# Hybrid decoder trunk: GpSimd's gathers of u and v in the order of the slots that use them, and the last norm in three parts

## The chip, the cores and the metric

The kernel runs on one core of one Trainium2 chip. The metric is device time in microseconds, from the start to the end of the program. The engines are TensorE (PE), VectorE (DVE), ScalarE (ACT), GpSimd (POOL) and SyncE (SP); each runs its own instructions in order, and they wait for each other by semaphores. 16 DMA engines serve the queues of SP and GpSimd.

## The reference

The model is a decoder trunk: 512 tokens, width 1024, two layers, float32. A layer has three token mixers, merged by gates, and then a layer of single-neuron experts (PEER); a last RMS norm closes it.

```python
for l in range(DEPTH):
    h = rmsnorm(x, norm1_g[l])
    z = h @ w_in[l]                                 # pool | ssm | q | k | v | 3 gates
    y_pool, y_ssm, y_attn = ...                     # pooling, state space, windowed attention
    merged = g[0] * y_pool + g[1] * y_ssm + g[2] * y_attn
    x = x + merged @ w_out[l]
    h2 = rmsnorm(x, norm2_g[l])
    x = x + peer_ffn(h2, ...)
return rmsnorm(x, final_g)
```

In the expert layer each token scores 128 + 128 keys for each of 8 heads, and keeps the 16 best pairs of a head: 128 experts of 16384 for a token. For every chosen expert e it computes a = h2 . u_tab[e], and adds gate * gelu(a) * v_tab[e] to the token. u_tab and v_tab hold a row of 1024 floats (4 KB) for each expert.

## The kernel before

**Tiles and picks.** Tokens go in tiles of 128, one to a partition; two layers of four tiles make eight tiles (TILES), numbered 0 to 7. A tile has 128 picks: in pick k every partition takes its own k-th expert. So there are 1024 picks, u picks and v picks alike, and for each one GpSimd issues an indirect DMA (L897) that gathers 128 rows of u (512 KB), and another for v. Rows of u land in one of six buffers (`rows_u`, pick mod 6), rows of v in one of six others (`rows_v`).

For a u pick VectorE multiplies the row with the token and sums (L2080, the dot; it bumps `dotted`). After each group of eight dots ACT takes the gelu (L1419) and VectorE multiplies by the gates (L2091, `weighed`). For a v pick, PE sums: ACT writes a diagonal matrix of the eight-group's weights (L1399, `diag_of`), and PE multiplies it with the rows of v into PSUM (L1147, `sum_pick`, two halves of 512 columns, each two matmuls in the trace). Some picks VectorE sums itself, into `tile_sum` (L1782; the first of a tile L1779). When a sum is done it bumps `v_free` of its buffer. At the end of a tile comes the "drain": VectorE joins both sums (L2059), PE transposes them (L951), and VectorE adds them to the tokens xT (L2066, `x_home`).

**The plan.** The order of all work is written at build time by `make_plan` as a list of slots; a slot takes at most one u pick and one v pick, and beside them pieces of the dense work ("items": projections, attention, selection of experts and so on, for a half of 256 tokens at a time) as far as assumed costs allow. Every engine then walks through the same slots in order. A v pick stands in the slot about 12 after the slot of its u pick (LAG): u picks fill slots 203 to 1226, v picks 215 to 1238. Dense items end near slot 1000; thereafter only picks are left, and all their v sums are PE's, because `v_on` asks for `at < len(order)`, that is, for dense items still to come.

**The gathers.** GpSimd walks through `GATHERS`, made by `gather_order`: the u pick of slot s is sorted under s, the v pick of slot s under s - 4 (V_AHEAD). Ahead of a u gather it waits for the dot of the pick six before (`dotted`), ahead of a v gather for the sum of the pick six before (`v_free`). The queue is in order: what stands behind a waiting gather waits too.

**Other traffic.** SP loads weights into a ring of six pieces of 512 KB, each once the piece six before is used.

**The last norm.** After the last slot the final norm is done for each half of 256 tokens in turn: ACT squares xT into hT (L1183), PE takes the mean with a matrix of ones (L1168), ACT the root (L1430), VectorE the reciprocal (L1898) and the scaling into hT (L1902, `scale`), SP stores hT (L803). Both halves use hT, so the second one's squares wait for the first one's store. Squares of the first half stand after all slots of ACT.

Of the kernel before, what the change touches and what calls it, by code (L numbers as in the profile page):

```python
# [12 lines left out]
ALU = mybir.AluOpType  # L13
# [3 lines left out]
P = 128  # L17
# [35 lines left out]
V_AHEAD = 4  # L53
# [106 lines left out]
def att_columns(T):  # L160
# [12 lines left out]
    "ptab": ("DVE",), "tb": ("PE", "ACT"), "wt": ("PE", "ACT", "DVE"), "drain": ("DVE", "PE", "DVE"), "store": ("DVE",),  # L173
}

# [4 lines left out]
def weight_of(item, part):  # L180

    kind, eng = item[0], CHAIN[item[0]][part]
    if eng == "PE":
        T = item[2] if kind in ("att_s", "att_p", "att_o") else 0
        return {"mean": (8, .43), "ssm_x": (8, .28), "ssm_y": (24, .28), "att_s": (1, .25 + .0017 * att_blocks(T) * 43), "att_p": (4, .28),
                "att_o": (att_blocks(T), .28), "mix": (2, .43), "glu_gate": (8, .43), "glu_val": (8, .43),
                "branch": (8 if item[-1] < 2 else 4, .43) if kind == "branch" else 0, "score": (4, .28), "htok": (4, .2),
                "tb": (4, .2), "wt": (16, .28), "masks": (2, .3), "drain": (8, .2)}.get(kind, (16, .43))
    if eng == "ACT":
        return {"squares": (4, .6), "mean": (1, .5), "ssm_u": (16, .29), "ssm_y": (16, .29), "q": (4, .6), "k": (4, .6),  # L190
                "att_e": (1, .25 + .0011 * att_blocks(item[2]) * P) if kind == "att_e" else 0, "att_o": (1, .3), "mix": (2, .4),
                "out": (1, .6), "pa": (2, .3), "wt": (3, .4), "settle": (1, .2), "angles": (2, .5), "score": (2, .38)}.get(kind, (1, .65))
    return {"mean": (9, .62), "ssm_x": (17, .43), "inject": (5, .2), "q": (3, .69), "k": (3, .69), "att_s": (1, .55),
            "att_e": (2, .24), "windows": (13, .55), "glu_val": (1, .7), "gate": (2 if kind == "gate" and item[3] else 1, .7),
            "out": (1, .7), "top": (22, .41), "settle": (3, .21), "angles": (12, .5), "masks": (10, .2), "pa": (45, .2),
            "pb": (44, .2), "pd": (8, .6), "ptb": (18, .55), "pca": (24, .55), "ptab": (75, .3), "wt": (4, .29),
            "drain": (2, .7)}.get(kind, (1, .3))
# [6 lines left out]
def prior(item):  # L204
# [187 lines left out]
def make_plan():  # L392
# [8 lines left out]
    shut = []  # L401

# [46 lines left out]
    while at < len(order) or v < TILES * PICKS or any(queue.values()) or shut:  # L449
# [5 lines left out]
        if v < u and v // GROUP * GROUP + GROUP <= u and (v // GROUP * GROUP + GROUP - 1) in end_of \  # L455
                and s - end_of[v // GROUP * GROUP + GROUP - 1] >= LAG - GROUP + 1 + v % GROUP:
            slot["v"] = v
            slot["v_on"] = "DVE" if v % PICKS % 2 == 1 and v % PICKS < PICKS - 1 and not queue["TOP"] and at < len(order) and (v < PICKS or ready([(("drain", v // PICKS - 1), 1)], s)) else "PE"
# [80 lines left out]
def trunk(nc, x_cm, positions, inv_freq, weights, keys, vecs, log_dt, ssm_bc, pool_edge, table_u, table_v, final_g, out_cm):  # L539
    par = nc.dram_tensor("ssm_par", (DEPTH * len(PARS) * P, BLK), F32)  # L540
    with ExitStack() as ctx:
# [202 lines left out]
        x_home = sem("x_home")  # L744
        final_ready = sem("final_ready")
# [26 lines left out]
        def run_sp(sp):  # L772
# [142 lines left out]
        def run_pe(pe):  # L915
# [29 lines left out]
            def emit(item, part):  # L945
                kind, u = item[0], item[1]
                if kind == "drain":
                    tile = item[1]
                    pe.wait_ge(sum_joined, 2 * (tile + 1))
                    for c in range(8):  # L950
                        mm = pe.transpose(ps[:, 4 + 2 * (tile % 2) + c // 4, (c % 4) * P:(c % 4 + 1) * P],  # L951
                                          tile_sum[:, c * P:(c + 1) * P], ident[:])
                        yield
                    mm.then_inc(sum_turned, 1)
                    return
# [209 lines left out]
            for half in range(2):  # L1165
                pe.wait_ge(squares_done, 4 * (2 * STAGES + half + 1))
                for k in range(KD):
                    mm = pe.matmul(ps[:, half, 0:N], mean_ones[:], hT[:, k, :], start=(k == 0), stop=(k == KD - 1))  # L1168
                mm.then_inc(tiles_done, 1)
# [3 lines left out]
        def run_act(act):  # L1173
# [12 lines left out]
            def emit(item, part):  # L1186
                kind, u = item[0], item[1]
                if kind == "squares":
# [6 lines left out]
                    yield from squares(u, norm_of(u, 0))  # L1195
                elif kind == "mean":
# [224 lines left out]
            for half in range(2):  # L1421
                act.wait_ge(x_home, 2 * (TILES - 2 + 2 * half))
                if half == 0:
                    act.wait_ge(tiles_done, len(RING_UNITS))
                else:
                    act.wait_ge(out_stored, 16)
                for _ in squares(half, 0):
                    pass
                act.wait_ge(tiles_done, len(RING_UNITS) + half + 1)
                act.activation(rms[:], ps[:, half, 0:N], ACT.Sqrt, bias=eps[:, 0:1]).then_inc(root_done, 1)  # L1430
# [3 lines left out]
        def run_dve(dve):  # L1434
# [460 lines left out]
            def scale(u, n, gain, dst):  # L1895
                t0 = N * (u % 2)
                dve.wait_ge(root_done, n + 1)
                dve.reciprocal(rstd[:], rms[:]).then_inc(normed, 1)  # L1898
                yield
                dve.wait_ge(normed, 9 * n + 1)  # L1900
                for k in range(KD):
                    dve.scalar_tensor_tensor(dst[:, k, :], xT[:, k, t0:t0 + N], gain[:, k:k + 1], rstd[:], ALU.mult,  # L1902
                                             ALU.mult).then_inc(normed, 1)
                    yield

            def emit(item, part):
                kind, u = item[0], item[1]
                if kind == "mean":
# [3 lines left out]
                    yield from scale(u, NORMS[item], vec[:, u // 2, at:at + KD], hT)  # L1912
# [202 lines left out]
            for half in range(2):  # L2115
                if half:
                    dve.wait_ge(out_stored, 16)
                for _ in scale(half, 2 * STAGES + half, fing, hT):
                    pass
                dve.wait_ge(normed, 9 * (2 * STAGES + half + 1))  # L2120
                dve.sem_inc(final_ready, 1)
# [98 lines left out]
```

## Time and profile before

| | us |
|---|---|
| median of three runs | 3755.12 (3745.66 to 3757.23) |
| profiled execution, its own time | 3761.48 |
| its span | 3759.7 |
| PE busy | 3216.2 (86%) |
| VectorE busy | 2533.9 (67%) |
| GpSimd busy | 2342.0 (62%) |
| ACT busy | 950.8 (25%) |
| moved by DMA | 1305.56 MB, 347 GB/s over the span |

Busy shares are means over parts with different limits, so the rows below are by stretch. A wait is told as the engine and line that waited, and what released it. A gather by GpSimd counts as busy while its instruction runs; the rows land later. In a timeline, "idle before" in brackets is the time in which the engine stood ahead of the row.

### The profile page before, as it was taken

Reading aid. Unit: us, or ns where it says so; the run is one execution under the profiler, and the core shown is the slowest. Engines: PE = TensorE matmul, PEld = TensorE weight load, DVE = VectorE, ACT = ScalarE, POOL = GpSimd, SP = SyncE. Lnnn points to the kernel's source line nnn. Section 1 sums busy time; section 2 is a strip of 40 time slices with the busy share of each in tenths; the row PEclk is TensorE's granted clock in tenths of the full one; section 3 lists DMA queues with packets and bytes.
Section 4 is the critical chain, followed back from the end, with each engine's and each line's share of the span. In section 5 each row is a group of like instructions: output and inputs, shape, how many; then the busy total and the mean of one; then the engine's idle time right before and its main releaser. Section 6 shows DMA issues by size and latency. Waiting matters only on the chain.

```text
span 3759.7 us, 37763 instructions
## 1 busy us (share of the span) xinstructions
PE 3216.2 (86%) x11496; PEld 2073.9 (55%) x11496; DVE 2533.9 (67%) x6139; ACT 950.8 (25%) x2095; POOL 2342.0 (62%) x2114
## 2 busy tenths in 40 slices
PE   8989899878988999867988999877988986777776
PEld 7778656445765656544765656544765642232233
DVE  6465788867566888766566888766566888444443
ACT  2331233323111243312111243323111222111111
POOL 1000476767667776666666776767666777777773
PEclk9989999989999999878999999989998988888888
DMA  5255799999999999999999999999999999999995
GB/s 176 90 202 202 289 381 386 380 356 357 401 386 384 385 382 381 377 347 338 395 387 384 395 385 379 374 342 355 395 400 372 390 340 349 362 373 369 365 365 216
DMA packets 361577, 1305.56 MB, mean 347 GB/s; under 512 B 40417, under 2 KB 42849, under 8 KB 361121
## 3 DMA queue, kind: packets, MB, share of 16 engines
q0 software_dynamic: 298960, 1087.79, 76.1%
q1 hardware_dynamic: 62416, 215.35, 15.1%
q8 instruction: 95, 1.56, 0.2%
q14 instruction: 106, 0.86, 0.1%
HBM read 1288.30 MB, written 14.68 MB: 347 GB/s over the span
## 4 chain that ended last, share of the span: by engine, by line
PE 36%; POOL 25%; DMA 17%; issue 12%; DVE 9%; another core or an unknown queue 1%; ACT 0%; DVEq 0%; SPq 0%; ACTq 0%; POOLq 0%
POOL heap L897 25%; DMA heap<-table_u,heap 17%; PE ps L1147 14%; PE ps L939 14%; DVE heap L2080 2%; PE ps L989 2%; DVE heap L1782 2%; PE ps L1084 1%; PE ps L1068 1%; PE ps L1034 1%; PE ps L1046 0%; PE ps L1028 0%; PE ps L970 0%; DMA ring<-ssm_par 0%
## 5 line engine op out<-in xcount | busy, mean ns | idle before, releaser
L1147 PE MATMUL ps<-heap 128*128 128x512 f32 x3268 | 1652.4, 645 | 352.3 <-ACT heap L1399 238.6
L2080 DVE CUSTOM_DVE_ANT_0 heap<-heap 128x1024 f32<-128x1024 f32 x1024 | 1251.5, 1222 | 946.6 <-DMA heap<-table_u,heap 879.6
L897 POOL DMA_INDIRECT heap<-table_v,heap x1024 | 1187.5, 1160 | 691.2 <-issue 265.2
L897 POOL DMA_INDIRECT heap<-table_u,heap x1024 | 1120.0, 1094 | 364.6 <-issue 312.1
L1147 PEld LDWEIGHTS ps<-heap 128*128 128x128 f32 x3268 | 653.7, 206 | 1046.6 <-issue 734.1
L939 PE MATMUL ps<-hT,ring 128*128 128x256 f32 x3840 | 895.6, 383 | 14.7 <-DVE hT L1902 9.8
L939 PEld LDWEIGHTS ps<-hT,ring 128*128 128x128 f32 x3840 | 735.1, 192 | 230.5 <-issue 133.3
L1399 ACT ACTIVATE heap<-ident,heap 128x128 f32<-128x128 f32 x817 | 292.4, 392 | 523.2 <-DVE heap L2091 275.2
L1782 DVE SCALAR_TENSOR_TENSOR heap<-heap 128x1024 f32<-128x1024 f32 x201 | 257.7, 1282 | 10.5 <-DVE stats L1949 4.5
L1419 ACT ACTIVATE heap<-heap 128x8 f32<-128x8 f32 x128 | 26.7, 208 | 941.2 <-DVE heap L2080 751.8
L1084 PE MATMUL ps<-temp,ring 128*128 128x256 f32 x640 | 151.7, 385 | 9.2 <-DVEq L1996 4.2
L939 PE MATMUL ps<-temp,ring 128*128 128x256 f32 x512 | 120.9, 396 | 27.8 <-DVE temp L1998 27.8
L1084 PEld LDWEIGHTS ps<-temp,ring 128*128 128x128 f32 x640 | 121.3, 192 | 39.7 <-issue 18.3
L939 PEld LDWEIGHTS ps<-temp,ring 128*128 128x128 f32 x512 | 101.9, 200 | 52.5 <-issue 38.2
L868 POOL DMA_DIRECT2D ssm_par<-heap x8 | 4.5, 564 | 185.3 <-DVEq L1644 185.3
L1419 ACT ACT_TABLE_LOAD x88 | 112.9, 1283 | 3.1
L1034 PE MATMUL ps<-temp 128*128 128x128 f32 x432 | 67.2, 314 | 35.4 <-DVE temp L1965 28.3
L1034 PEld LDWEIGHTS ps<-temp 128*128 128x128 f32 x432 | 63.7, 225 | 57.2 <-issue 56.6
L989 PE MATMUL ps<-ring,hT 128*128 128x256 f32 x384 | 89.3, 380 | 0.0
L1304 ACT ACTIVATE temp<-ps 128x512 f32<-128x512 f32 x48 | 28.6, 597 | 236.7 <-PE ps L939 236.3
L1238 ACT ACTIVATE temp<-ps 32x512 f32<-32x512 f32 x96 | 56.5, 589 | 125.9 <-PE ps L939 116.8
L989 PEld LDWEIGHTS ps<-ring,hT 128*128 128x128 f32 x384 | 72.8, 190 | 25.4 <-issue 17.2
(255 smaller groups left out, 2588.5 us busy)
## 6 DMA issues: line engine op xcount, KB each, us to landing
ring<-weights SPq DMA_DIRECT2D x344, 512.0 KB
ring<-ssm_par SPq DMA_DIRECT2D x48, 512.0 KB
heap<-table_u,heap POOLq DMA_INDIRECT x1024
heap<-table_v,heap POOLq DMA_INDIRECT x1024
ssm_par<-heap POOLq DMA_DIRECT2D x20, 512.0 KB, 6.2
ring<-weights SPq DMA_DIRECT2D x20, 256.0 KB
xT<-x_cm SPq DMA_DIRECT2D x2, 1024.0 KB, 9.6
ssm_par<-heap POOLq DMA_DIRECT2D x8, 256.0 KB, 2.8
```

Source lines behind the costliest of these rows:

```text
L897: pool.indirect_dma_start(rows[:, j, :], None, table, bass.IndirectOffsetOnAxis(expert[:, tile % 2, k:k + 1], 0)).then_inc(landed, 16)
L939: mm = pe.matmul(ps[:, b, i * width:(i + 1) * width], piece(u, name, k * P, P), src[:, k, :], start=(k == 0), stop=(k == rows_n - 1))
L989: mm = pe.matmul(ps[:, b, tt * 256:(tt + 1) * 256], hT[:, k, tt * P:(tt + 1) * P], piece(u, names[k // 4], (k % 4) * 256, 256), start=(k = ...
L1034: mm = pe.matmul(ps[:, b, (j % 4) * P:(j % 4 + 1) * P], srow[:, j * P:(j + 1) * P], weigh_d, start=True, stop=True)
L1068: mm = pe.matmul(ps[:, b, j * N:(j + 1) * N], piece(u, name, (4 * j + k) * P, P), ssmT[u][:, k, :], start=(k == 0), stop=(k == 3))
L1084: mm = pe.matmul(ps[:, b, j * N:(j + 1) * N], piece(u, ("branch", mm2, br), (rows_n * j + k) * P, P), src[:, k, :], start=(k == 0), stop=( ...
L1147: mm = pe.matmul(ps[:, 4 + 2 * (tile % 2) + half, :], diag[:, PE_TURN[v] % DIAGS, :], rows_v[:, v % NV, half * 512:(half + 1) * 512], star ...
L1238: ins = act.activation(turn_s[to, :], ps[at:at + 32, b, :], ACT.Copy, scale=1.0 if q % 2 else -1.0)
L1399: act.activation(diag[:, n % DIAGS, :], ident[:], ACT.Copy, scale=w_st[:, g % 3, v % GROUP:v % GROUP + 1]).then_inc(diag_ready, 1)
L1419: act.activation(gelu_st[:, n % 3, :], act_st[:, n % 3, :], ACT.Gelu_apprx_tanh).then_inc(gelued, 1)
L1782: dve.scalar_tensor_tensor(tile_sum, rows_v[:, v % NV, :], w, tile_sum, ALU.mult, ALU.add).then_inc(v_free[v % NV], 1)
L2080: dve.tensor_tensor_reduce(row, row, h_tok[:, tile % 2, :], 1.0, 0.0, ALU.mult, ALU.add, act_st[:, g % 3, pick % GROUP:pick % GROUP + 1]). ...
```

## The change

`gather_order` sorts both picks of a slot under the slot; within one slot u comes first. V_AHEAD is gone. The final norm becomes a kind of item, "final", in three parts (`FINALS`): tokens 0 to 255 once tile 5 has drained, 256 to 383 once tile 6 has, and 384 to 511 once tile 7 has. Their pieces stand in the plan like others, so the first two fall into slots in which picks of tiles 6 and 7 are at work. Each part waits for the store of the part before, since all use hT. Of the last 24 v picks, odd ones may be VectorE's.

```diff
-V_AHEAD = 4
+    "final": ("ACT", "PE", "ACT", "DVE"),
+FINALS = ((TILES - 3, 0, N), (TILES - 2, N, P), (TILES - 1, N + P, P))
...
+    if kind == "final":
+        return [end("htok", STAGES - 1, 1, 1)] + ([end("final", u - 1)] if u else [])
...
-            slot["v_on"] = "DVE" if v % PICKS % 2 == 1 and v % PICKS < PICKS - 1 and not queue["TOP"] and at < len(order) and (...) else "PE"
+            slot["v_on"] = "DVE" if v % PICKS % 2 == 1 and v % PICKS < PICKS - 1 and not queue["TOP"] and (at < len(order) or v >= TILES * PICKS - 24) and (...) else "PE"
...
+        while finals and ready([(("drain", FINALS[finals[0]][0]), 2)] + prior(("final", finals[0])), s):
+            enqueue(("final", finals.popleft()), 0, s)
...
         if slot["v"] is not None:
-            out.append((s - V_AHEAD, "v", slot["v"]))
+            out.append((s, "v", slot["v"]))
...
-            for half in range(2):
-                sp.wait_ge(final_ready, half + 1)
-                sp.dma_start(out_cm[:, half, :].rearrange("p (k t) -> p k t", t=N), hT[:]).then_inc(out_stored, 16)
-            sp.wait_ge(out_stored, 32)
+            for n, (_, t0, width) in enumerate(FINALS):
+                sp.wait_ge(final_ready, n + 1)
+                sp.dma_start(out_cm[:, t0 // N, :].rearrange("p (k t) -> p k t", t=N)[:, :, t0 % N:t0 % N + width],
+                             hT[:, :, t0 % N:t0 % N + width]).then_inc(out_stored, 16)
+            sp.wait_ge(out_stored, 16 * len(FINALS))
...
+                if kind == "final":
+                    t0, width = FINALS[u][1] % N, FINALS[u][2]
+                    pe.wait_ge(bank_free[u], BANK_TOTAL[u])
+                    pe.wait_ge(squares_done, 4 * (2 * STAGES + u + 1))
+                    for k in range(KD):
+                        mm = pe.matmul(ps[:, u, 0:width], mean_ones[:], hT[:, k, t0:t0 + width], start=(k == 0), stop=(k == KD - 1))
...
+                elif kind == "final":
+                    tile, t0, width = FINALS[u]
+                    if part == 0:
+                        act.wait_ge(x_home, 2 * (tile + 1))
+                        if u == 0:
+                            act.wait_ge(tiles_done, len(RING_UNITS))
+                        else:
+                            act.wait_ge(out_stored, 16 * u)
+                        for i in range(4):
+                            act.activation(hT[:, 2 * i:2 * i + 2, t0 % N:t0 % N + width], xT[:, 2 * i:2 * i + 2, t0:t0 + width],
+                                           ACT.Square).then_inc(squares_done, 1)
+                            yield
+                    else:
+                        act.wait_ge(final_mean, u + 1)
+                        act.wait_ge(normed, 9 * (2 * STAGES + u))
+                        act.activation(rms[:, 0:width], ps[:, u, 0:width], ACT.Sqrt, bias=eps[:, 0:1]).then_inc(root_done, 1)
...
+                elif kind == "final":
+                    _, t0, width = FINALS[u]
+                    yield from scale(t0, width, 2 * STAGES + u, fing)
+                    dve.wait_ge(normed, 9 * (2 * STAGES + u + 1))
+                    dve.sem_inc(final_ready, 1)
```

The loops over two halves that stood behind the slots of PE, ACT and VectorE are taken out.

## Rows read from the trace of the kernel before

**Rows 1.** The page: chain by engine and by line, and one costly group.
```profile
PE 36%; POOL 25%; DMA 17%; issue 12%; DVE 9%; another core or an unknown queue 1%; ACT 0%; DVEq 0%; SPq 0%; ACTq 0%; POOLq 0%
POOL heap L897 25%; DMA heap<-table_u,heap 17%; PE ps L1147 14%; PE ps L939 14%; DVE heap L2080 2%; PE ps L989 2%; DVE heap L1782 2%; PE ps L1084 1%; PE ps L1068 1%; PE ps L1034 1%; PE ps L1046 0%; PE ps L1028 0%; PE ps L970 0%; DMA ring<-ssm_par 0%
...
L1782 DVE SCALAR_TENSOR_TENSOR heap<-heap 128x1024 f32<-128x1024 f32 x201 | 257.7, 1282 | 10.5 <-DVE stats L1949 4.5
```

**Rows 2.** Stretches: busy PE, PEld, DVE, ACT, POOL; granted clock; DMA share; GB/s.
```profile
500.00:700.00 200.00, 196.57 (x660) 121.79 (x660) 170.84 (x503) 72.33 (x168) 137.60 (x122) 0.98 0.99 379
700.00:900.00 200.00, 156.23 (x612) 96.88 (x613) 142.71 (x288) 61.26 (x120) 139.76 (x119) 0.86 0.96 357
900.00:1100.00 200.00, 189.03 (x765) 139.83 (x764) 122.06 (x187) 46.07 (x82) 134.65 (x120) 0.98 1.01 398
1880.00:1940.00 60.00, 58.90 (x239) 45.04 (x238) 37.02 (x54) 12.33 (x21) 37.54 (x35) 1.00 1.03 409
500.00:3100.00 2600.00, 2300.59 (x8266) 1495.74 (x8267) 1889.66 (x4423) 707.71 (x1519) 1785.51 (x1564) 0.93 0.98 376
3100.00:3700.00 600.00, 429.05 (x843) 179.56 (x841) 309.68 (x660) 87.07 (x254) 445.87 (x416) 0.85 0.97 364
```

**Rows 3.** Groups, 500 to 3100 us: busy, mean ns, idle before, its releasers.
```profile
L1147 PE MATMUL ps<-heap 128*128 128x512 f32 x2306 | 1165.1, 635 | 179.0 <-ACT heap L1399 152.2 <-DMA heap<-table_v,heap 18.0 <-issue 8.5
L2080 DVE CUSTOM_DVE_ANT_0 heap<-heap 128x1024 f32<-128x1024 f32 x783 | 956.6, 1222 | 653.5 <-DMA heap<-table_u,heap 601.2 <-issue 45.4 <-ACT heap L1419 1.0
L897 POOL DMA_INDIRECT heap<-table_v,heap x782 | 912.5, 1167 | 576.0 <-PE ps L1147 206.0 <-issue 190.1 <-DVE heap L1782 167.0
```

**Rows 4.** Groups from the start to 1500 us: how many had begun.
```profile
L2080 DVE CUSTOM_DVE_ANT_0 heap<-heap 128x1024 f32<-128x1024 f32 x333 | 406.7, 1221 | 237.6 <-DMA heap<-table_u,heap 220.2 <-issue 14.9 <-DVE stats L1949 0.4
L897 POOL DMA_INDIRECT heap<-table_u,heap x336 | 371.8, 1107 | 154.9 <-issue 102.4 <-DVE heap L1891 51.3 <-DVE heap L2080 1.2
```

**Rows 5.** Groups, 3100 to 3700 us.
```profile
L2080 DVE CUSTOM_DVE_ANT_0 heap<-heap 128x1024 f32<-128x1024 f32 x209 | 255.9, 1225 | 283.2 <-DMA heap<-table_u,heap 268.5 <-issue 14.7
L897 POOL DMA_INDIRECT heap<-table_v,heap x208 | 239.6, 1152 | 90.9 <-issue 67.5 <-remote 16.3 <-PE ps L1147 7.2
L897 POOL DMA_INDIRECT heap<-table_u,heap x208 | 206.5, 993 | 63.4 <-issue 63.4
```

**Rows 6.** Timeline in the tail: start us, us, engine, line, idle before.
```profile
3562.43 0.94 POOL L897 DMA_INDIRECT heap<-table_u,heap  x1 [0.30 <-issue]
3563.15 1.22 DVE L2080 CUSTOM_DVE_ANT_0 heap<-heap 128x1024 f32<-128x1024 f32 x1 [1.82 <-DMA heap<-table_u,heap]
3563.68 1.51 POOL L897 DMA_INDIRECT heap<-table_v,heap  x1 [0.31 <-issue]
```

**Rows 7.** Timeline after the last dot: PE's sums, and its weight loads.
```profile
3704.54 0.08 DVE L2080 DVE_READ_ACCUMULATOR2_ANT heap<- 128x1 f32 x1
...
3705.21 21.49 PE L1147 MATMUL ps<-heap 128*128 128x512 f32 x44 [6.21 <-ACT heap L1399]
3706.23 0.34 PEld L1147 LDWEIGHTS ps<-heap 128*128 128x128 f32 x1 [0.52 <-issue]
...
3710.66 0.19 PEld L1147 LDWEIGHTS ps<-heap 128*128 128x128 f32 x1 [0.24 <-issue]
```

**Rows 8.** Timeline of the end.
```profile
3726.74 1.29 DVE L2059 COPY heap<-ps 128x512 f32<-128x512 f32 x2 [21.54 <-PE ps L1147]
...
3729.21 1.28 DVE L2066 TENSOR_TENSOR xT<-xT,ps 128x512 f32<-128x512 f32 x2 [1.19 <-PE ps L951]
...
3744.49 5.19 PE L1168 MATMUL ps<-hT,mean_ones 128*128 128x256 f32 x16 [11.86 <-ACT hT L1183]
3749.71 0.47 ACT L1430 ACTIVATE rms<-ps,eps 128x256 f32<-128x256 f32 x1 [5.28 <-PE ps L1168]
3750.29 1.75 DVE L1898 RECIPROCAL rms<-rms 128x256 f32<-128x256 f32 x1 [12.07 <-ACT rms L1430]
3752.08 3.26 DVE L1902 SCALAR_TENSOR_TENSOR hT<-xT,fing,rms 128x256 f32<-128x256 f32 x8
```

More of the change, by code:

```diff
@@ L172 @@
     "settle": ("DVE", "ACT"), "angles": ("DVE", "ACT"), "masks": ("PE", "DVE"), "pa": ("DVE", "ACT"), "pb": ("DVE",), "pd": ("DVE",), "ptb": ("DVE",), "pca": ("DVE",),
-    "ptab": ("DVE",), "tb": ("PE", "ACT"), "wt": ("PE", "ACT", "DVE"), "drain": ("DVE", "PE", "DVE"), "store": ("DVE",),
+    "ptab": ("DVE",), "tb": ("PE", "ACT"), "wt": ("PE", "ACT", "DVE"), "drain": ("DVE", "PE", "DVE"),
+    "final": ("ACT", "PE", "ACT", "DVE"),
 }
+FINALS = ((TILES - 3, 0, N), (TILES - 2, N, P), (TILES - 1, N + P, P))
 RINGED = ("masks", "mean", "ssm_u", "ssm_x", "ssm_y", "q", "k", "v", "att_s", "att_p", "att_o", "pool_u", "mix", "glu_gate", "glu_val",
@@ L187, in weight_of @@
                 "branch": (8 if item[-1] < 2 else 4, .43) if kind == "branch" else 0, "score": (4, .28), "htok": (4, .2),
-                "tb": (4, .2), "wt": (16, .28), "masks": (2, .3), "drain": (8, .2)}.get(kind, (16, .43))
+                "tb": (4, .2), "wt": (16, .28), "masks": (2, .3), "drain": (8, .2), "final": (8, .4)}.get(kind, (16, .43))
     if eng == "ACT":
-        return {"squares": (4, .6), "mean": (1, .5), "ssm_u": (16, .29), "ssm_y": (16, .29), "q": (4, .6), "k": (4, .6),
+        return {"squares": (4, .6), "final": (4 if part == 0 else 1, .6), "mean": (1, .5), "ssm_u": (16, .29), "ssm_y": (16, .29), "q": (4, .6), "k": (4, .6),
                 "att_e": (1, .25 + .0011 * att_blocks(item[2]) * P) if kind == "att_e" else 0, "att_o": (1, .3), "mix": (2, .4),
@@ L196, in weight_of @@
             "pb": (44, .2), "pd": (8, .6), "ptb": (18, .55), "pca": (24, .55), "ptab": (75, .3), "wt": (4, .29),
-            "drain": (2, .7)}.get(kind, (1, .3))
+            "drain": (2, .7), "final": (9, .5)}.get(kind, (1, .3))
 def final_part(kind):
@@ L401, in make_plan @@
     shut = []
+    finals = deque(range(len(FINALS)))
     def ready(keys, s):
@@ L448, in make_plan @@
     s = 0
-    while at < len(order) or v < TILES * PICKS or any(queue.values()) or shut:
+    while at < len(order) or v < TILES * PICKS or any(queue.values()) or shut or finals:
         slot = {"u": None, "v": None, "PE": [], "ACT": [], "DVE": []}
@@ L457, in make_plan @@
             slot["v"] = v
-            slot["v_on"] = "DVE" if v % PICKS % 2 == 1 and v % PICKS < PICKS - 1 and not queue["TOP"] and at < len(order) and (v < PICKS or ready([(("drain", v // PICKS - 1), 1)], s)) else "PE"
+            slot["v_on"] = "DVE" if v % PICKS % 2 == 1 and v % PICKS < PICKS - 1 and not queue["TOP"] and (at < len(order) or v >= TILES * PICKS - 24) and (v < PICKS or ready([(("drain", v // PICKS - 1), 1)], s)) else "PE"
         busy = slot["u"] is not None or slot["v"] is not None
@@ L744, in trunk @@
         x_home = sem("x_home")
+        final_mean = sem("final_mean")
         final_ready = sem("final_ready")
@@ L1164, in run_pe @@
             assert not live
[L1165 to L1169, printed above, removed]
         def run_act(act):
@@ L1420, in run_act @@
             assert not live
[L1421 to L1430, printed above, removed]
         def run_dve(dve):
@@ L1893, in settle, with scale @@
                 yield
-            def scale(u, n, gain, dst):
-                t0 = N * (u % 2)
+            def scale(t0, width, n, gain):
                 dve.wait_ge(root_done, n + 1)
-                dve.reciprocal(rstd[:], rms[:]).then_inc(normed, 1)
+                dve.reciprocal(rstd[:, 0:width], rms[:, 0:width]).then_inc(normed, 1)
                 yield
@@ L1901, in scale @@
                 for k in range(KD):
-                    dve.scalar_tensor_tensor(dst[:, k, :], xT[:, k, t0:t0 + N], gain[:, k:k + 1], rstd[:], ALU.mult,
-                                             ALU.mult).then_inc(normed, 1)
+                    dve.scalar_tensor_tensor(hT[:, k, t0 % N:t0 % N + width], xT[:, k, t0:t0 + width], gain[:, k:k + 1],
+                                             rstd[:, 0:width], ALU.mult, ALU.mult).then_inc(normed, 1)
                     yield
@@ L1911, in emit @@
                     at = V_G2 if item[2] else V_G1
-                    yield from scale(u, NORMS[item], vec[:, u // 2, at:at + KD], hT)
+                    yield from scale(N * (u % 2), N, NORMS[item], vec[:, u // 2, at:at + KD])
+                elif kind == "final":
[3 more added lines that the diff above has]
+                    dve.sem_inc(final_ready, 1)
                 elif kind == "ssm_x":
@@ L2114, in run_dve @@
             assert not live and not pending
[L2115 to L2121, printed above, removed]
         with nc.Block() as block:
```

5 lines of the change are left out of this document (added).

## The prediction

> **What bounds the kernel now.** I read the page first, then the stretches, the waits, and last the end of the timeline. The page calls PE 86% busy (the table above), and the chain that ended last lies on PE for 36%, on GpSimd's gathers for 25% and on u rows in flight for 17% [rows 1]. No engine alone is the bound, so the time must be read by stretch [rows 2]: a body (500 to 3100 us) where the dense stages and the expert picks run together, a tail (3100 to 3700) with picks alone, and the last 60 us.
>
> In the body the DMA engines look full (share 0.98), but the rate tells more than the share: 376 GB/s on average, 357 in one stretch of 200 us, 398 in another and 409 over the 60 us from 1880. So "busy" at 376 is not full. The reader should see next who is late [rows 3]: VectorE waits 601.2 us for rows of u, PE only 18.0 us for rows of v. GpSimd, which asks for both in one order, itself waits 206.0 us for PE and 167.0 us for VectorE's sums, 373 us together. By the code those are waits for a free v buffer: a gather of v is asked four slots early, so with six buffers it can't go out before the sum of two slots back is done, and the next u queues behind it. The counts show the result: at 1500 us 336 gathers of u had been asked for and 333 dots had begun [rows 4]; at eight other times from 1000 to 3400 us the lead was one to three. There are six u buffers, and these few are used to cover the flight, while v lies waiting.
>
> In the tail GpSimd bounds: 208 pairs take 446.1 us of gathers and 130.9 us of issue gaps, 577 of 600; only 23.5 us are waits for a sum ("remote" counted as one) [rows 5].
>
> **The order of the gathers, in the body.** Nothing is added or removed; there are as many gathers, of 512 KB each. v of a slot now follows u of the same slot, so GpSimd waits for the dot and the sum of six slots back. Both may be up to six slots ahead, and the 373 us of waits should mostly go, then the 601 us. What is late next? The body moves 2600 x 376 = 978 MB, which at 409 GB/s is 2390 us; PE has 2301 us of work; GpSimd has 2600 - 373 = 2227; VectorE 1890. So DMA at its real limit comes next: the gain is at most 210 us. It will be less, since the bounds alternate: in four of the thirteen stretches of 200 us PE is busy for 189 us or more (500 to 700: 196.6, and 900 to 1100: 189.0 are shown), and six slots of buffer, some 20 us, can't carry work from one stretch to the next. Taking for each stretch the larger of PE's work and its bytes at 404 GB/s (a little under the best, for 200 us) gives, for the three shown, 196.6, 176.7 and 197.0 of 200, and over all thirteen about 2436: 164 us to be had. I take half, **80 us**, because at a grain of 20 us PE's bursts leave less. Nearest rows for the ends: nothing gained (DMA share is already 0.98) and 210.
>
> The price: v loses its lead of four slots. It was hardly needed: a row of v is asked for four slots, about 13 us, before its slot and then has to wait for it. With both six ahead, PE waits for v as rarely as now. If u and v came no earlier than u does now, PE would take VectorE's wait; that is the rival below.
>
> The Trainium skill ("DMA: Bandwidth & Descriptors", Specifications) gives about 358 GB/s as the HBM limit for one core. By it the body, at 376, would have nothing left to gain. The trace disagrees: 398 GB/s over 200 us and 409 over 60 [rows 2].
>
> **The tail.** GpSimd stays the bound. Its 23.5 us of waits should go, since VectorE's and PE's six buffers are never all held there: **-20 us**, between 0 and -23.5. Its gathers don't get shorter. One that starts while a dot runs is held: the dot from 3563.15 ends at 3564.37 and the gather that began at 3563.68 ends 0.82 later, after 1.51 us; free ones take 0.94 [rows 6]. A pair costs 0.94 + 0.94 + 2 x 0.30 = 2.48 us free and 2.77 (577/208) as measured. As dots start on a row's landing in both versions, I leave this at nothing; if every second gather met a fresh dot (1.9 us at worst) it would cost up to 0.4 us per slot, +80.
>
> The skill ("SBUF — State Buffer", SBUF: two separate sides) says that a VectorE operation with two SBUF inputs and a GpSimd one exclude each other for a whole instruction. The trace shows the hold, but from inside the dot only; a gather begun ahead of a dot keeps 0.94 us. By the page's rule a pair beside a dot would take 1.88 + 0.60 + 1.22 = 3.7 us; it takes 2.77.
>
> PE sums every pick of the tail in four matmuls, 0.43 us each at 2.4 GHz and 0.85 at 1.2 (a weight load and the gap behind it: 0.19 + 0.24, 0.34 + 0.52) [rows 7], so 1.71 or 3.42 us a pick against slots of 2.86. The granted clock is 0.85 there: PE races ahead on v rows at hand, then stands until a group's gelu, 6 to 7 us. With v arriving at the pace of u its gaps are shorter and spread out, and the clock should hold or rise. Bound of harm: all at 1.2 GHz, 208 x (3.42 - 2.86) = +116.
>
> **The last picks.** After the last dot (ends 3704.6) PE sums twelve picks alone, in 21.5 us for 44 matmuls, while VectorE stands 21.5 us [rows 7, 8]. Eleven of the last 24 picks now go to VectorE, five of them among those twelve (1013 to 1021, odd; 1023 stays on PE). PE drops 5 x 1.71 = 8.6 us; VectorE's 5 x 1.28 [rows 1] fit beside. GpSimd then has to feed eight gathers at 1.24 and a flight of some 4: 14 us, about what PE needs (7 x 1.71 = 12, and the clock's start). **-8 us**, 0 to -10.
>
> **The last norm.** From x home (3730.5) to the end are 29.2 us: two outputs of 256 tokens in series, since both go through hT [rows 8]. Now 384 tokens are normed in the tail, and 128 stay: squares 4 x 0.38 = 1.5 (256 elements; Sqrt of 256 takes 0.47), 16 matmuls of 128 columns at 0.18 = 2.9 (0.33 for 256 in the slow state), Sqrt 0.4, reciprocal half of 1.75 = 0.9, scaling 8 x 0.25 = 2.0, output 3.9 falling to about 3.2, handoffs 0.4: 11.3. **-18 us**, -16 to -20. What moved ahead costs VectorE 5.0 + 2.6 us, ACT some 6, PE some 8, and 1.5 MB (4 us at 400 GB/s): VectorE has 268.5 us of waits for u in the tail to hide it [rows 5]; ACT is 15% busy. ACT's wait for the first output stands ahead of the diagonals that PE needs, but some hundred slots lie between the two parts. +1 us; 5 if the cover fails.
>
> Sum: -80 - 20 - 8 - 18 + 1 = **-125 us**. The profiled execution took 3761.5 (span 3759.7 and 1.8 around it), so 3636.5; it was 6.4 above the median of the three runs, 3755.1, so the median of after is **3630**.
>
> **Rivals.**
> A. The DMA is as full as it gets (share 0.98, and every stretch shown from 500 to 3700 us at 0.96 or more); deeper queues only lengthen the flight. For it: the share. Against it: 409 GB/s at 1.03. The page's 358 GB/s would say the same. Then only tail, picks and norm are left: 3755 - 45 = **3710**.
> B. The looser loop gives nearly all of the 210: PE's own time shrinks too, as the body's clock (0.93) rises. For it: in the 700 to 900 stretch PE works 156 of 200 us at clock 0.86. Then 3755 - 210 - 45 = 3500 at best, **3540** with the grain of PE's bursts.
> C. Slower: v becomes as late as u. This needs GpSimd's lead to stay at one to three slots, which is so if its pair (2.85 us in the body: 2227/782) can't outrun slots of 3.3, or if each head of the line is held by PE. PE then waits on rows of v as VectorE does on u, ahead of dense matmuls that stages wait for. PE's idle 300 us absorb the first part; it decides from waits of 345 us (300, and the 45 gained elsewhere). With the full 601, 3755 + 301 - 45 = 4011; midway, **3880**. A PE held at 1.2 GHz in the tail belongs here as well: 3755 + 116 - 25 = 3846.
>
> **Chances.** Forecast 0.62; A 0.19; B 0.10; C 0.09, of which 0.03 ends within the bound of no change. That bound is 0.3%, 11 us, about what runs of this kernel can tell. The forecast's own range is 3580 to 3690. For eight in ten I leave out C and the best of B: 3550 to 3725. A, B and the forecast all are faster by more than 11 us: 0.91; same 0.03; slower 0.06.
>
> **What would show it.** VectorE's wait for u in the body falls from 601 to under 350; GpSimd's waits for PE and for VectorE's sums from 373 to under 150; the body's rate rises from 376 to about 388; more gathers of u than dots by four to six at a given time. In the tail, slots of about 2.77. One output DMA of half size after the last x home, some 11 us from the end. I am wrong if GpSimd's waits stay, if PE waits for v by hundreds of us, or if the rate rises and the time doesn't.

## The result, and the profile after

| | before | after |
|---|---|---|
| median | 3756.18 (4 runs) | 3549.03 (4 runs) |
| range | 3745.66 to 3761.63 | 3546.22 to 3563.16 |
| profiled span | 3759.7 | 3561.4 |

The ratio is 0.9465 (95% interval 0.9446 to 0.9483), 207 us by the medians. The direction was right, the size was not: the forecast said 126 us, and the time came out near where rival B had put it (3540): 31 us below the forecast's own range (3580 to 3690) and one below the range of eight in ten (3550 to 3725).

I read the profile after in the order used before. The page, then the stretches (busy PE, PEld, DVE, ACT, POOL; granted clock; DMA share; GB/s), which answer to [rows 1, 2]:

```profile
POOL 36%; PE 31%; issue 13%; DMA 12%; DVE 8%; ACT 0%; DVEq 0%; SPq 0%; POOLq 0%; ACTq 0%
POOL heap L906 36%; PE ps L948 14%; DMA heap<-table_v,heap 11%; PE ps L1166 11%; DVE heap L2105 2%; PE ps L1008 2%; DVE heap L1803 1%; PE ps L1103 1%; PE ps L1047 1%; PE ps L1087 0%; DMA ring<-ssm_par 0%; PE ps L1149 0%; PE ps L1053 0%; PE ps L1019 0%; PE ps L1065 0%
```

```profile
500.00:700.00 200.00, 198.73 (x681) 124.78 (x682) 173.37 (x514) 73.45 (x170) 141.17 (x126) 1.00 1.01 393
700.00:900.00 200.00, 171.91 (x690) 105.32 (x691) 158.36 (x320) 67.23 (x133) 154.89 (x131) 0.91 1.01 396
900.00:1100.00 200.00, 184.34 (x727) 135.18 (x726) 120.03 (x184) 42.81 (x73) 142.13 (x122) 0.97 1.02 399
500.00:3000.00 2500.00, 2298.26 (x8367) 1489.70 (x8368) 1918.31 (x4568) 727.13 (x1551) 1848.53 (x1598) 0.96 1.02 399
3000.00:3480.00 480.00, 348.54 (x734) 122.79 (x732) 255.18 (x515) 82.11 (x222) 371.84 (x356) 1.00 1.01 389
```

The body now ends near 3000 us. Its rate is 399 GB/s instead of 376, and the stretch from 700 us, which stood at 357, moves 396: the slack places filled most. Rows in flight have changed table in the chain, too: 17% for u then, 11% for v now. The groups of the body, 500 to 3000 us (busy, mean ns | idle before, what ended it), answer to [rows 3]:

```profile
L1166 PE MATMUL ps<-heap 128*128 128x512 f32 x2375 | 1179.1, 625 | 184.5 <-DMA heap<-table_v,heap 172.9 <-ACT heap L1430 11.2
L2105 DVE CUSTOM_DVE_ANT_0 heap<-heap 128x1024 f32<-128x1024 f32 x800 | 969.9, 1219 | 61.7 <-DMA heap<-table_u,heap 54.0 <-DVE stats L1974 2.3 <-DVE temp L2012 1.8
L906 POOL DMA_INDIRECT heap<-table_u,heap x799 | 935.8, 1171 | 309.7 <-issue 227.3 <-DVE heap L2105 82.4
L906 POOL DMA_INDIRECT heap<-table_v,heap x799 | 914.1, 1144 | 342.0 <-issue 202.6 <-PE ps L1166 138.3 <-DVE heap L2105 1.1
L1803 DVE SCALAR_TENSOR_TENSOR heap<-heap 128x1024 f32<-128x1024 f32 x201 | 258.1, 1284 | 342.7 <-issue 229.7 <-DMA heap<-table_v,heap 108.5 <-DVE stats L1974 2.2
```

800 dots in 2500 us are 3.13 us each; before, 783 in 2600 were 3.32. VectorE's wait for u fell from 601 us to 54, and in its place PE waits 173 for rows of v and VectorE's sums stand idle for 343, of which 108 are put down to v. The wait for u has in part changed its name, then: ahead of dots and sums together VectorE stood 664 us (653.5 and 10.5) and now stands 404 (61.7 and 342.7). GpSimd still waits 222 us for a free buffer. Its lead at 1500 us [rows 4] is six:

```profile
L2105 DVE CUSTOM_DVE_ANT_0 heap<-heap 128x1024 f32<-128x1024 f32 x345 | 418.7, 1219 | 25.1 <-DMA heap<-table_u,heap 22.1 <-DVE stats L1974 1.0 <-DVE temp L2012 0.6
L906 POOL DMA_INDIRECT heap<-table_u,heap x351 | 405.2, 1154 | 186.1 <-issue 99.0 <-DVE heap L1912 52.0 <-DVE heap L2105 35.0
```

That moment is a high one. Counted every half microsecond from 500 to 2900 us, gathers of u are 4.5 ahead of dots in the mean, between three and six for 98% of the time; before, 2.5.

The tail from 3000 to 3480 us [rows 5]: GpSimd waits for nobody, its gathers and issue gaps fill 480.6 of 480 us, and the clock is 1.00 instead of 0.85.

```profile
L2105 DVE CUSTOM_DVE_ANT_0 heap<-heap 128x1024 f32<-128x1024 f32 x180 | 220.2, 1225 | 222.4 <-DMA heap<-table_u,heap 222.3
L906 POOL DMA_INDIRECT heap<-table_v,heap x178 | 193.1, 1085 | 54.2 <-issue 54.2
L906 POOL DMA_INDIRECT heap<-table_u,heap x178 | 179.1, 1006 | 54.2 <-issue 54.2
```

The end [rows 7, 8], with VectorE's sums (L1803) among the last gathers:

```profile
3524.90 5.17 PE L1166 MATMUL ps<-heap 128*128 128x512 f32 x8 [3.37 <-DMA heap<-table_v,heap]
...
3530.19 1.28 DVE L1803 SCALAR_TENSOR_TENSOR heap<-heap 128x1024 f32<-128x1024 f32 x1 [2.11 <-DMA heap<-table_v,heap]
3530.30 1.99 POOL L906 DMA_INDIRECT heap<-table_v,heap  x1 [0.30 <-issue]
...
3537.09 0.98 POOL L906 DMA_INDIRECT heap<-table_v,heap  x1 [0.30 <-issue]
...
3541.32 3.67 PE L1166 MATMUL ps<-heap 128*128 128x512 f32 x8 [1.35 <-DMA heap<-table_v,heap]
...
3547.49 1.28 DVE L2091 TENSOR_TENSOR xT<-xT,ps 128x512 f32<-128x512 f32 x2 [1.19 <-PE ps L960]
3548.82 1.33 ACT L1219 ACTIVATE hT<-xT 128x256 f32<-128x256 f32 x4 [14.72 <-DVE xT L2091]
...
3550.29 3.75 PE L970 MATMUL ps<-hT,mean_ones 128*128 128x128 f32 x16 [2.83 <-ACT hT L1219]
3554.08 0.37 ACT L1225 ACTIVATE rms<-ps,eps 128x128 f32<-128x128 f32 x1 [2.63 <-PE ps L970]
3554.48 0.95 DVE L1918 RECIPROCAL rms<-rms 128x128 f32<-128x128 f32 x1 [5.70 <-ACT rms L1225]
3555.47 2.19 DVE L1922 SCALAR_TENSOR_TENSOR hT<-xT,fing,rms 128x128 f32<-128x128 f32 x8
```

Where the 198.3 us between the two profiled spans lie, read from the starts of single dots in the timelines:

| us | before | after | difference |
|---|---|---|---|
| start to the first dot | 409.7 | 416.5 | +6.8 |
| dots 0 to 100 | 316.6 | 303.1 | -13.5 |
| dots 100 to 830 | 2425.4 | 2283.7 | -141.7 |
| dots 830 to 1000 (picks alone) | 487.8 | 455.9 | -31.9 |
| dot 1000 to the end of the last dot | 65.1 | 65.6 | +0.5 |
| to PE's last sum | 22.1 | 20.3 | -1.8 |
| to the last x home | 3.8 | 3.8 | 0 |
| to the end | 29.2 | 12.6 | -16.6 |

### The profile page after: what moved, and what is told of

It is laid out like the page before. It is cut to its first block, busy times and chain, and to the rows that moved or that the text cites. A ratio compares the mean times of both kernels' runs of the same rounds, so it can differ in the third digit from the quotient of the medians.

```text
span 3561.4 us, 37721 instructions
## 1 busy us (share of the span) xinstructions
PE 3145.3 (88%) x11468; PEld 2012.2 (57%) x11468; DVE 2528.4 (71%) x6159; ACT 962.3 (27%) x2092; POOL 2364.8 (66%) x2114
## 4 chain that ended last, share of the span: by engine, by line
POOL 36%; PE 31%; issue 13%; DMA 12%; DVE 8%; ACT 0%; DVEq 0%; SPq 0%; POOLq 0%; ACTq 0%
POOL heap L906 36%; PE ps L948 14%; DMA heap<-table_v,heap 11%; PE ps L1166 11%; DVE heap L2105 2%; PE ps L1008 2%; DVE heap L1803 1%; PE ps L1103 1%; PE ps L1047 1%; PE ps L1087 0%; DMA ring<-ssm_par 0%; PE ps L1149 0%; PE ps L1053 0%; PE ps L1019 0%; PE ps L1065 0%
## 5 line engine op out<-in xcount | busy, mean ns | idle before, releaser
L1166 PE MATMUL ps<-heap 128*128 128x512 f32 x3224 | 1599.1, 623 | 345.1 <-DMA heap<-table_v,heap 285.2
L906 POOL DMA_INDIRECT heap<-table_u,heap x1024 | 1162.6, 1135 | 436.2 <-issue 293.7
L906 POOL DMA_INDIRECT heap<-table_v,heap x1024 | 1167.6, 1140 | 410.6 <-issue 271.2
L1166 PEld LDWEIGHTS ps<-heap 128*128 128x128 f32 x3224 | 597.7, 196 | 1047.7 <-issue 782.7
L1803 DVE SCALAR_TENSOR_TENSOR heap<-heap 128x1024 f32<-128x1024 f32 x211 | 271.0, 1284 | 362.9 <-issue 242.6
L2105 DVE DVE_READ_ACCUMULATOR2_ANT heap<- 128x1 f32 x1024 | 84.0, 82 | 0.0
L1349 ACT COPY temp<-ps 128x512 f32<-128x512 f32 x32 | 18.7, 586 | 220.9 <-PE ps L948 220.9
```

Of the source, the lines that this page charges most:

```text
L906: pool.indirect_dma_start(rows[:, j, :], None, table, bass.IndirectOffsetOnAxis(expert[:, tile % 2, k:k + 1], 0)).then_inc(landed, 16)
L1166: mm = pe.matmul(ps[:, 4 + 2 * (tile % 2) + half, :], diag[:, PE_TURN[v] % DIAGS, :], rows_v[:, v % NV, half * 512:(half + 1) * 512], star ...
L1803: dve.scalar_tensor_tensor(tile_sum, rows_v[:, v % NV, :], w, tile_sum, ALU.mult, ALU.add).then_inc(v_free[v % NV], 1)
L2105: dve.tensor_tensor_reduce(row, row, h_tok[:, tile % 2, :], 1.0, 0.0, ALU.mult, ALU.add, act_st[:, g % 3, pick % GROUP:pick % GROUP + 1]). ...
```

## The experiments

Twelve kernels ran, in three lots; those of a lot share a chip and its runs of the kernel before, to which the ratios are (95% interval in brackets). The kernel before had medians of 3756.05, 3748.62 and 3749.72 in them. The columns on the right are of each one's profile: GB/s and picks (dots) between 500 and 2900 us, where the kernels before and after have 376 GB/s with 718 dots, and 400 with 766.

| run | median us | ratio | GB/s | dots |
|---|---|---|---|---|
| order alone | 3562.39 | 0.949 [0.947, 0.951] | 399 | 764 |
| order back | 3728.25 | 0.994 [0.991, 0.996] | 376 | 718 |
| no VectorE sums in the last picks | 3548.29 | 0.946 [0.944, 0.947] | 400 | 766 |
| VectorE sums from pick 1012 | 3540.43 | 0.944 [0.942, 0.946] | 399 | 766 |
| v two ahead | 3570.24 | 0.951 [0.947, 0.954] | 397 | 761 |
| v four ahead, 4 u and 8 v buffers | 3585.70 | 0.956 [0.952, 0.960] | 396 | 757 |
| slot order, 4 and 4 | 3672.19 | 0.978 [0.974, 0.983] | 384 | 733 |
| slot order, 3 and 3 | 3986.06 | 1.063 [1.058, 1.067] | 348 | 666 |
| the changed kernel again | 3554.08 | 0.947 [0.944, 0.949] | 399 | 765 |
| v one ahead, sums from 1012 | 3531.70 | 0.942 [0.940, 0.944] | 402 | 771 |
| the same, 5 u and 7 v buffers | 3538.42 | 0.943 [0.941, 0.946] | 401 | 769 |
| half weights | 3502.12 | 0.933 [0.930, 0.935] | 379 | 783 |

### The two parts of the change

**Order alone**, on the kernel before:

```diff
-V_AHEAD = 4
+V_AHEAD = 0
```

> The kernel before with V_AHEAD = 0 and nothing else: both picks of a slot are asked for under the slot. Theory (the lead of the gathers): this edit carries what the prediction mis-sized, so about 3575 us (the changed kernel's 3549 plus some 25 for the norm and the last picks), body at about 400 GB/s, VectorE's wait for u in the body under 100 us, the tail's slots 2.70 us with clock near 1. Rival (the norm's new place and the last picks matter as much as the order): 3640 or more, body near 385 GB/s.

**Order back**, on the changed kernel:

```diff
-            out.append((s, "v", slot["v"]))
+            out.append((s - 4, "v", slot["v"]))
```

> The changed kernel with v asked for four slots ahead again; the norm in three parts and VectorE's sums in the last picks stay. Theory: body and tail as in the kernel before (376 GB/s, u waited for about 600 us), the end shorter by the norm's 17 us and a few of the picks: 3730 to 3740. Rival (the parts need each other): 3700 or less, or no gain at all over 3756.

Measured: 193.7 us for the order, 27.8 for the rest; together 221, where the whole change gave 207. On top of the order the rest gives about 13 us (3562 to 3549), not 28, and the intervals of these two overlap. The order is the change: alone it brings VectorE's wait for u in the body (500 to 2900 us) down to 58 us.

```profile
L2080 DVE CUSTOM_DVE_ANT_0 heap<-heap 128x1024 f32<-128x1024 f32 x764 | 925.4, 1218 | 65.6 <-DMA heap<-table_u,heap 58.2 <-DVE stats L1949 2.3 <-DVE temp L1987 1.8
```

With the order turned back the groups of the body are those of before to a few per cent, though everything else is new. Two lines of the kernel before, 500 to 2900 us, and the same two of "order back":

```profile
L2080 DVE CUSTOM_DVE_ANT_0 heap<-heap 128x1024 f32<-128x1024 f32 x718 | 877.4, 1222 | 624.0 <-DMA heap<-table_u,heap 572.8 <-issue 44.5 <-ACT heap L1419 1.0
L897 POOL DMA_INDIRECT heap<-table_v,heap x717 | 840.1, 1172 | 545.2 <-PE ps L1147 194.6 <-issue 170.7 <-DVE heap L1782 167.0
```

```profile
L2105 DVE CUSTOM_DVE_ANT_0 heap<-heap 128x1024 f32<-128x1024 f32 x718 | 877.5, 1222 | 624.4 <-DMA heap<-table_u,heap 618.9 <-DVE stats L1974 0.4 <-DVE temp L1728 0.4
L906 POOL DMA_INDIRECT heap<-table_v,heap x717 | 844.8, 1178 | 524.9 <-PE ps L1166 195.8 <-DVE heap L1803 172.8 <-issue 149.3
```

### Is it the lead, or the early v?

With four slots ahead and six buffers the gather of v waits for the sum two slots back, and so the u behind it in the queue for a sum three back. Four edits of the kernel before change this number without, or with, the slot order (NU and NV stand in lines of their own; the last column writes two kernels in one, with 4, and with 3, of each).

```diff
 # v two ahead                # four ahead, 4 and 8       # slot order, 4 and 4 (3 and 3)
-V_AHEAD = 4                  -NU = 6                     -V_AHEAD = 4
+V_AHEAD = 2                  +NU = 4                     +V_AHEAD = 0
                              -NV = 6                     -NU = NV = 6
                              +NV = 8                     +NU = NV = 4 (3)
```

> The kernel before with V_AHEAD = 2 in place of 4. Theory (lead): what counts is how many slots back the sum or dot lies for which the next u gather has to wait in the queue. It is 3 in the kernel before (the v gather ahead of it waits for the sum two slots back), 6 or 7 with V_AHEAD = 0, and 5 here; a row takes 7 to 9 us, some 2.5 to 3 slots. So most of the gain is there already: 3580 to 3610. Rival (asking for v early is itself the harm, in proportion): halfway, 3660.

> The kernel before with V_AHEAD = 4 kept, but four buffers for u and eight for v (NU = 4, NV = 8), twelve together as before. The v gather of four slots ahead then waits for the sum four slots back. Theory (lead): the queue's distance is 4 instead of 3, so clearly faster than 3756 with the early v kept and two u buffers fewer: 3620 to 3660, and like the kernel with four and four in slot order. Rival (the early v itself is the harm): 3756 or slower, as u has fewer buffers.

> The kernel before with V_AHEAD = 0 and only four buffers each (NU = NV = 4). Theory (lead): distance 4 for both; 3620 to 3660, still far below 3756 with a third fewer buffers. Rival (twelve buffers of rows in flight or at hand are what fills the DMA): 3750 or slower.

> The kernel before with V_AHEAD = 0 and three buffers each (NU = NV = 3). Theory (lead): distance 3, as in the kernel before, which has twice the buffers: 3750 to 3850, VectorE and PE both waiting for rows. Rival (slot order alone is the gain, whatever the depth): near 3562.

Count for each table how many slots may lie between asking and using. The kernel before has 3 for u and 6 for v, the changed one 6 and 6, "two ahead" 5 and 6, "4 and 8" 4 and 8, the last two 4 and 4, 3 and 3.

The rival "asking early is the harm" falls with "4 and 8": v is asked for four slots ahead there as before, u has fewer buffers, and it is 163 us faster than the kernel before. The rival "slot order alone" falls with "3 and 3", which is 237 us slower. The kernel "4 and 4" beats the one before with eight buffers against twelve. So the lead it is, and that of both tables. From 3 and 6 to 4 and 4, u's lead grows by one and v's shrinks by two, and 76 us are gained; with u's left at 4, v's going from 4 to 8 gives 86 more; with u's left at 3, v's going from 6 to 3 costs 237 (the order changes there too). Counted in the traces as above, gathers of u are ahead of dots by 2.3 in "3 and 3", 2.5 before, 3.0 in "4 and 4", 3.1 in "4 and 8", 3.6 in "two ahead" and 4.5 after.

But my numbers missed in two places. I had the two kernels with a lead of four alike, at 3620 to 3660; they are 86 us apart (3586 and 3672), and with three and three I expected 3750 to 3850 where 3986 came. In the body of "3 and 3" (first), against that of "4 and 8":

```profile
L2080 DVE CUSTOM_DVE_ANT_0 heap<-heap 128x1024 f32<-128x1024 f32 x666 | 809.6, 1221 | 260.6 <-DMA heap<-table_u,heap 254.1 <-DVE stats L1949 2.3 <-DVE temp L1974 0.6
L1147 PE MATMUL ps<-heap 128*128 128x512 f32 x1952 | 1046.1, 664 | 366.6 <-DMA heap<-table_v,heap 344.1 <-ACT heap L1399 19.6 <-issue 2.2
```

```profile
L2080 DVE CUSTOM_DVE_ANT_0 heap<-heap 128x1024 f32<-128x1024 f32 x757 | 924.1, 1222 | 473.4 <-DMA heap<-table_u,heap 466.2 <-DVE stats L1949 1.0 <-DVE xT L2006 0.6
L1147 PE MATMUL ps<-heap 128*128 128x512 f32 x2192 | 1073.0, 618 | 109.8 <-ACT heap L1399 100.7 <-DMA heap<-table_v,heap 9.1
```

The slow kernel has less waiting ahead of dots (261 us against 473), but VectorE stands another 455 us ahead of its sums of v, against 10.5, and PE, which is the busier engine, waits 344 us for v where the other waits 9. That is rival C of the prediction, made real by a small lead. The early v had a value, then; the mistake of the kernel before was to pay for it with u's lead. Whether a late v costs more than a late u, no run here separates.

### The last picks

On the changed kernel; the second has 12 in place of 24.

```diff
-... not queue["TOP"] and (at < len(order) or v >= TILES * PICKS - 24) and ...
+... not queue["TOP"] and at < len(order) and ...
```

> The changed kernel with all of the last 24 v picks on PE again. My prediction gave VectorE's eleven sums 8 us. The trace after shows last dot to last sum at 20.3 us against 22.1, and slots of about 2.9 us for the twelve last u picks where VectorE sums, against 2.6 just before. Theory now: what PE saves after the last dot is paid ahead of it, by dots that stand behind a late v row, so within 4 us of 3549. Rival (the prediction): slower by 8 us, 3557.

> The changed kernel with VectorE's sums only from pick 1012 on, that is in the twelve slots after the last dot. Theory (VectorE's sums cost where they stand ahead of a dot and save where no dot is left): 3 to 6 us faster than the changed kernel, 3544. Rival (gathers of the last rows set the end, whoever sums them): the same as without any, within 1 us of it.

Without VectorE's sums: 3548.3, the same as the changed kernel. With sums in the last twelve slots alone: 3540.4; its interval and that of the run without overlap (0.9418 to 0.9463, 0.9442 to 0.9470), so 8 us of gain are likely and not shown. The timelines agree with the theory in kind. The stretch from dot 1000 to the last dot's end takes 65.6 us with sums from 1000 on (67.1 in the repeat), 60.2 without, 60.6 with twelve; from there to PE's last sum are 20.3 (19.5), 22.7 and 20.3. The five to seven us paid ahead of the last dot are more than the two or three saved behind it.

### Is the body at the DMA's limit, and is there something better?

The repeat is the changed kernel itself. "v one ahead" sorts v under s - 1 and starts VectorE's last sums at pick 1012; its sister has NU = 5 and NV = 7. "Half weights" leaves out half of each weight piece from the 24th on:

```diff
-... else BLK
+... else (BLK if c < 4 * RING else BLK // 2)
```

> The changed kernel once more, beside the three that are compared with it, on their chip: 3540 to 3565, and its tail's slots between 2.58 and 2.70 us.

> The changed kernel with v asked for one slot ahead, and VectorE's sums from pick 1012 on. In the changed kernel the wait for u in the body is 54 us, but PE and VectorE wait for rows of v for 150 us and more. Theory (lead): a slot more for v costs u one of seven slots of distance, which the run with two ahead showed to be cheap; v's waits shrink by half and the body gains up to 1%: 3520 to 3540. Rival (the DMA is at its limit in the body, 400 of 409 GB/s): within 5 us of the changed kernel but for the last picks.

> As the kernel with one slot ahead, but five buffers for u and seven for v. Theory (lead): u at five slots back, v at six with one ahead; both about as early as the flight asks: 3520 to 3540, a little better than six and six. Rival (limit): the same as the changed kernel, and the only gain is that of the last picks.

> The changed kernel with half of each weight piece left out of its transfer (from the 24th piece on; 512 columns of 1024, the rest of the ring keeps what stood there), so its output is not the reference's. About 85 MB less, of which some 68 MB fall into the body. Theory (the body is at the DMA's limit now): 60 to 140 us faster than the changed kernel, PE's 92% being the next bound. Rival (PE, or the coupling of the engines' orders, bounds the body now): less than 20 us.

One ahead is the fastest of all, 3531.7, 22 us under the changed kernel beside it (0.9419 [0.9396, 0.9442] against 0.9468 [0.9443, 0.9492]: the intervals just part). Dots 100 to 830 take 2266 us instead of 2286. Its waits in the body tell that a slot was moved from u to v: VectorE waits 363.5 us for u again, but its sums stand 53 us in place of 343, which makes 421 ahead of both, against 404. So the name of the wait moved, and its length hardly.

```profile
L2105 DVE CUSTOM_DVE_ANT_0 heap<-heap 128x1024 f32<-128x1024 f32 x771 | 941.3, 1221 | 367.7 <-DMA heap<-table_u,heap 363.5 <-DVE stats L1974 1.0 <-DVE xT L2031 0.6
L1803 DVE SCALAR_TENSOR_TENSOR heap<-heap 128x1024 f32<-128x1024 f32 x201 | 258.1, 1284 | 53.2 <-issue 30.5 <-DMA heap<-table_v,heap 9.5 <-DVE stats L1974 4.7
```

Of the 22 us, some 9 by the timelines belong to the last picks (from dot 1000 to PE's last sum 78.0 us, in the repeat 86.6), and what the body gains, dots 830 to 1000 give back in part (454.5 against 443.5). The five and seven split is no better.

Half the weights gave 52 us, below the 60 to 140 of one theory and above the 20 of the other. Between 500 and 2900 us:

```profile
500.00:2900.00 2400.00, 2246.29 (x8271) 1471.30 (x8270) 1869.38 (x4414) 714.78 (x1523) 1822.46 (x1560) 0.96 0.99 379
```

against 2220.41 us of PE and 400 GB/s in the changed kernel. The rate falls back from 400, and PE gets busier, to 94%. Neither theory holds alone; I read it as a body that has come close to both bounds at once. How much each is worth stays open.

## Why the prediction was right in kind and small in size

**The loop of the body: right, and mis-sized.** GpSimd's waits for a v buffer, and the u queued behind them, were what bound, as "order alone" shows. The number of slots between asking and using went from three to six, and the wait for u went, to 54 us (I asked for under 350). The term was 80 us; measured are 155 (dots 0 to 830). The step that failed is "I take half, because at a grain of 20 us PE's bursts leave less". The bound by stretches of 200 us had been 164 us, and 155 is 95% of it. But the bound itself had moved, so that six slots carried work over PE's bursts is argued and not shown. I took PE's busy time as a fixed amount of work: while it did 783 picks' worth of body in 2301 us before, 800 took 2298, as the granted clock rose from 0.93 to 0.96. That is 2.94 and 2.87 us a pick, some 50 us over the body. The 404 GB/s that I took for every stretch were not reached in the mean, which is 399, though the stretch from 1900 to 2100 us moves 409.

GpSimd's own waits were to fall under 150 us and stand at 222. I read them as another kind, waits for a buffer six slots back with six rows asked for. "Half weights" tells them apart in part: with less to move, GpSimd's wait for dots falls from 84 us to 5, while its wait for PE's sums stays at 130 (138), so the second doesn't hang on a full DMA. My sign for "right" was badly chosen there.

**The price of v: wrong as put.** "With both six ahead, PE waits for v as rarely as now": it waits 173 us instead of 18, and VectorE's sums wait too. PE's waits for ACT's diagonals went from 152 us to 11 at the same time, so its idle time ahead of the sums is the same in all (179.0 and 184.5), and PE stayed 92% busy (2298 of 2500).

**The tail: right on the bound, wrong on the gathers' length.** I took -20 us for the waits and nothing for the length of gathers, "as dots start on a row's landing in both versions". Measured is -32 in the profiled execution of after (dots 830 to 1000), and its kin with the same order do better: 441 us in "order alone" and 444 in the repeat where before has 488, so about -45. The waits were 17 us there; most of the rest is shorter gathers, 12 us in after and 28 in "order alone". A gather that starts while a dot runs is held until 0.82 us after the dot's end [rows 6], and what counts is how late in the dot it starts. When its pair and the dots fall into step, gathers start past the dot or near its end. Counted over dots 860 to 1000, 71 of the 281 gathers took over 1.05 us before, 23 of 280 in "order alone". In step (the changed kernel without VectorE's last sums):

```profile
3466.02 1.01 POOL L906 DMA_INDIRECT heap<-table_u,heap  x1 [0.31 <-issue]
3466.39 1.95 PE L1166 MATMUL ps<-heap 128*128 128x512 f32 x4 [0.61 <-ACT heap L1430]
3467.33 0.94 POOL L906 DMA_INDIRECT heap<-table_v,heap  x1 [0.30 <-issue]
3467.55 1.22 DVE L2105 CUSTOM_DVE_ANT_0 heap<-heap 128x1024 f32<-128x1024 f32 x1 [1.33 <-DMA heap<-table_u,heap]
3468.58 1.01 POOL L906 DMA_INDIRECT heap<-table_u,heap  x1 [0.31 <-issue]
3468.95 1.95 PE L1166 MATMUL ps<-heap 128*128 128x512 f32 x4 [0.61 <-ACT heap L1430]
```

From one gather of u to the next are 2.56 us (0.94, 1.01, and two gaps of 0.30 to 0.31). Eight of the eleven profiles in which GpSimd never waits in the tail have 2.58 or 2.59 us a slot over dots 860 to 1000, the other three 2.63 to 2.67; the three in which it does wait have 2.87 (before), 2.78 ("order back") and 2.83 ("3 and 3"). So a wait seems to throw the pair out of step, and costs more than its own length. But the step isn't there from the start either: without any wait the changed kernel runs at 2.7 to 2.9 us a slot to dot 920, but for one group of ten dots, and at 2.54 to 2.62 from there, in the repeat from dot 870. What brings it about stays open. The slow PE clock is not what keeps it away, as "4 and 8" shows: v is early there and PE runs in bursts as before, at a clock of 0.87, and yet its tail has slots of 2.58 us and moves 402 GB/s, with no wait of GpSimd for a sum (3018 to 3478 us of a span of 3579):

```profile
3018.00:3478.00 460.00, 357.45 (x714) 150.28 (x713) 245.38 (x484) 70.54 (x208) 352.58 (x353) 0.87 1.02 402
L897 POOL DMA_INDIRECT heap<-table_u,heap x177 | 182.8, 1033 | 54.0 <-issue 54.0
L897 POOL DMA_INDIRECT heap<-table_v,heap x176 | 170.4, 968 | 53.6 <-issue 53.6
```

The Trainium skill ("SBUF — State Buffer", SBUF: two separate sides) lets an operation of VectorE with two SBUF inputs and one of GpSimd that reads SBUF exclude each other for a whole instruction, whichever starts first. The trace agrees one way round, also for VectorE's sums: the gather that begins at 3530.30 inside a sum takes 1.99 us. It doesn't the other way: dots take 1.22 us and sums 1.28, gather or no gather.

**The clock: as foretold.** With v rows at the pace of u, PE's gaps in the tail are about 0.6 us in place of 6, and the granted clock is 1.00 instead of 0.85. It gave no time there, as "4 and 8" shows.

**The last picks: wrong.** Of -8 us, -1.3 came, and against the changed kernel without these sums they cost 3 us by the timelines (85.9 from dot 1000 to PE's last sum, 82.9 without). I had counted PE's five sums, and put the gathers at 14 us; from the last dot's end (3524.7) to the start of PE's last two sums (3541.3) are 16.6, PE waiting for rows of v each time, and the gathers that begin inside a VectorE sum are held (1.99, 1.94, 1.71, 1.59). Ahead of the last dot, the sums delay dots by five us. With v early again ("order back") the stretch from the last dot to PE's last sum falls by 5.0 us, 22.1 to 17.1: it is the rows that are late.

**The last norm: right.** 11.3 us were foretold for the part that stays and 12.6 came (PE's 16 matmuls 3.75 us for 2.9); -16.6 for -18. The parts in the tail cost little: dots 830 to 1000 take 441 us in "order alone", which has none of them, and 444 and 441 in the changed kernel without VectorE's last sums and with twelve of them.

**The rivals.** B was nearest, for the reason it gave: the looser loop took nearly all of the stretch bound, and PE's work shrank. It had 170 us for the body, where 155 came, and 45 for the rest, where the profile has 43; that those 43 fit is luck, since the tail gave more than foretold and the last picks next to nothing. A falls: 399 to 409 GB/s at a share of 1.02 to 1.03 where 376 stood at 0.98. With A falls the limit of 358 GB/s that the prediction took from the Trainium skill ("DMA: Bandwidth & Descriptors", Specifications). C didn't happen here, but "3 and 3" shows that its mechanism is real, at 1.063.

## What to carry to other kernels

When one in-order queue feeds two consumers, count for each how many steps back the queue has to wait for a buffer; prefetching one table early can cut the lead of the other, because the other stands behind it. A busy share of 0.98 on the DMA engines is no proof of a limit: compare its GB/s with the best stretch of the same trace. A wait of an engine that serves both consumers can move from one to the other, so add up its waits before calling one of them gone. And where a bound is worked out from stretches, halving it by feel is no estimate: here 95% of it came.

## What the runs showed of the hardware

Gathers by GpSimd and VectorE's dots can lock into step: 2.56 us for a pair and a dot of 1.22, against 2.87 in the tail of before, where they don't. The DMA engines' busy share can read above 1, and small steps of it go with large ones of the rate: 0.98 went with 376 GB/s, 1.02 with 399, 1.03 with 409. Between two executions of the changed kernel dots 830 to 1000 took 456 and 444 us, which is 12 us of the 21 over which its times spread (3542 to 3563).
